# Four long bursts of compression matmuls in place of nine short ones, between the k-tiles of an NSA projection

## The reference

```python
L_CMP = 32
def nsa_project(h, w_in, pos):
    z = h @ w_in                      # D_MODEL = 1024 in, q, kc, vc, ks, vs, kw, vw and gates out
    ...
def nsa_compress(k, pe, w):           # k: (B, L, NSA_KV, NSA_DH)
    blk = k.reshape(B, L // L_CMP, L_CMP, NSA_KV, NSA_DH) + pe[:, None, :]
    return jnp.einsum('bclgd,lde->bcge', blk, w)
```

## Time and profile before

| what | value |
|---|---|
| median of 3 runs | 3520.2 us |
| profiled execution | 3519.06 us |
| span of its trace | 3517.4 us |
| PE busy | 3184.3 us (91%) |
| DVE, ACT, POOL busy | 1839.1, 1292.3, 386.6 us |
| mean granted TensorE clock | 0.957 |
| DMA | 339.10 MB, mean 96 GB/s |

### The profile page before, as it was taken

One profiled execution on the slowest core, in us unless ns is written; L12 is line 12 of the kernel. 1 busy time (PEld: TensorE's weight loads), 2 busy tenths in 40 slices (PEclk: granted clock), 3 DMA queues, 4 the chain that ended last, 5 costly groups with the idle time before them and its releaser, 6 DMA issues. The chain is left out here.

```text
span 3517.4 us, 71223 instructions
## 1 busy us (share of the span) xinstructions
PE 3184.3 (91%) x29474; PEld 2946.8 (84%) x29474; DVE 1839.1 (52%) x3124; ACT 1292.3 (37%) x2225; POOL 386.6 (11%) x266
## 2 busy tenths in 40 slices
PE   7988889999889678778999898999989989889997
PEld 6875579999789678668999897999988855789997
DVE  2136636546489654436636484764622256356363
ACT  3236524323355323024323374432322256343232
POOL 2222110000134000020000032000012221200000
PEclk9999999999999899789999999999999999999999
DMA  6634222232222000214222322323265443042322
GB/s 188 198 112 165 93 101 88 84 105 72 67 77 74 5 0 0 84 66 149 80 101 83 85 90 84 111 84 102 74 142 167 142 163 115 31 149 75 105 83 67
DMA packets 146424, 339.10 MB, mean 96 GB/s; under 512 B 58212, under 2 KB 84452, under 8 KB 132468
## 3 DMA queue, kind: packets, MB, share of 16 engines
q1 hardware_dynamic: 137204, 296.03, 26.4%
q0 software_dynamic: 7424, 37.76, 2.9%
q10 hardware_dynamic: 1536, 1.60, 0.2%
HBM read 318.40 MB, written 32.12 MB: 100 GB/s over the span
## 5 line engine op out<-in xcount | busy, mean ns | idle before, releaser
L357 PE MATMUL ffn_ps<-ffn_x_hi_sb,ffn_w_hi_sb 128*128 128x260 f32 x2816 | 571.9, 284 | 40.8 <-DVE ffn_x_lo_sb L165 37.5
L357 PE MATMUL ffn_ps<-ffn_x_hi_sb,ffn_w_lo_sb 128*128 128x260 f32 x2816 | 569.5, 284 | 0.0
L357 PE MATMUL ffn_ps<-ffn_x_lo_sb,ffn_w_hi_sb 128*128 128x260 f32 x2816 | 568.8, 284 | 0.0
L357 PEld LDWEIGHTS ffn_ps<-ffn_x_hi_sb,ffn_w_hi_sb 128*128 128x128 f32 x2816 | 436.7, 190 | 46.1 <-issue 35.8
L357 PEld LDWEIGHTS ffn_ps<-ffn_x_hi_sb,ffn_w_lo_sb 128*128 128x128 f32 x2816 | 436.4, 189 | 0.0
L357 PEld LDWEIGHTS ffn_ps<-ffn_x_lo_sb,ffn_w_hi_sb 128*128 128x128 f32 x2816 | 435.4, 189 | 0.0
L397 ACT ACTIVATE ffn_w_hi_sb<-ffn_raw_sb 128x2048 fp32r<-128x2048 f32 (+2 forms) x152 | 256.9, 1690 | 349.1 <-PE ffn_ps L357 349.1
L449 DVE TENSOR_TENSOR ffn_w_lo_sb<-ffn_raw_sb,ffn_w_hi_sb 128x2048 fp32r<-128x2048 f32 (+2 forms) x152 | 305.1, 2007 | 47.3 <-ACT ffn_w_hi_sb L397 47.3
L415 ACT ACTIVATE ffn_pre_sb<-ffn_ps 128x520 f32<-128x520 f32 x176 | 106.6, 606 | 605.4 <-PE ffn_ps L357 315.9
L464 DVE SCALAR_TENSOR_TENSOR ffn_conv_sb<-ffn_pre_sb,ffn_conv_w_sb,ffn_conv_sb 128x512 f32<-128x512 f32 x176 | 132.3, 752 | 344.9 <-ACT ffn_conv_sb L417 344.9
L357 PE MATMUL ffn_ps<-ffn_inner_hi_sb,ffn_w_hi_sb 128*128 128x260 f32 x1408 | 283.9, 283 | 6.5 <-DVE ffn_inner_lo_sb L482 3.4
(11 more groups left out here) (451 smaller groups left out, 6335.4 us busy)
## 6 DMA issues: line engine op xcount, KB each, us to landing
ffn_raw_sb<-ffn_w_in SPq DMA_DIRECT2D x88, 1024.0 KB, 4.9
ffn_raw_sb<-ffn_w_out SPq DMA_DIRECT2D x32, 768.0 KB, 4.3
nsa_ring_sb<-sel_pages SPq DMA_DIRECT2D x160, 128.0 KB, 2.5
ffn_raw_sb<-ffn_w_out SPq DMA_DIRECT2D x32, 640.0 KB, 3.9
nsab_w_raw_sb<-nsa_w_in SPq DMA_DIRECT2D x32, 512.0 KB, 5.3
nsab_page_slot_sb<-cmp_pages SPq DMA_DIRECT2D x64, 256.0 KB, 3.9
all_xn_t_sb<-cmp_pages SPq DMA_DIRECT2D x64, 256.0 KB, 3.6
gdnp_w_raw_sb<-gdn_w_in SPq DMA_DIRECT2D x32, 512.0 KB, 3.9
```

The costliest lines, as they stand in the source:

```text
L357: mm = pe.matmul(psf[:, bank + h, 0:H], wp[:, w[0], w[1]:w[1] + P], xp[:, h * H:(h + 1) * H], start=start and k == 0, stop=stop and k == 2)
```

## The change

The number of compression steps that shall be done by k-tile `step` (0 to 10) of group n was a straight line from step 1 to step 10, and becomes four equal jumps of eight:

```diff
--- before.py
+++ after.py
@@ -1754,7 +1754,7 @@
                     if u >= FIRST:
                         n, step = (u - FIRST) * KT + kt, 0
                         n, step = n // STEPS, n % STEPS
-                        compress_to(32 * n + max(0, step - 1) * 32 // (STEPS - 2))
+                        compress_to(32 * n + 8 * sum(step >= at for at in (3, 5, 8, 10)))
```

## The result

The changed kernel takes 3499.24 us, median of six runs (3496.48 to 3503.0), against 3520.46 us (3518.35 to 3525.12, six runs). The ratio is 0.9938 with a 95% interval of [0.9926, 0.9951]: 21.2 us less, where 28 were forecast. The median lies 0.2 us above the upper end of the stated range (3499). The profiled execution took 3496.48 us (span 3494.8), 22.6 us less than the profiled one of before.

A forecast was written before the change was run, and what follows sets the result against it. The prediction took PE (TensorE) to bound the stretch: 80 fewer switches at 0.357 us save 28.6 us, less a 0.65 us page wait gives 27.95 us, so 3492.0 us from a median of 3520.2, range 3489 to 3499.

The forecast's parts named there:

- PE bounds the stretch: Units 5 to 15 of both NSA projections: PE busy 119.19 of 119.63 and 118.58 of 118.86 us, so its savings count.
- The price of a switch, 0.357 us: Each compression burst between projection k-tiles: fixed 0.357 us for switching there and back, whatever the burst's length.
- The term of 28.6 us: Compression bursts in both layers: 80 fewer, at 0.357 us each, save 28.6 us.
- Longer bursts keep their pace: Bursts of 64 matmuls in the trace: still 0.117 us a compression step, 1.10 us to the next projection matmul.
- Weights and ACT's copies don't bind: Shorter units: weight loads hold 5.74 us a unit, shortest unit 8.3 us; ACT gets 0.72 us more for copies.
- A page wait of 0.65 us: Group 5's first burst: sample 4's last page late, 0.35 us in layer 0 plus 0.3 in layer 3; bounds 0 to 4.
- the third rival: Long bursts starve PE of instructions: last 8 matmuls slow to 120 ns, 46.6 us lost, 3539 us; chance 0.05.
- The range: Whole kernel: 3489 (full 28.6 us, cheaper remaining switches) to 3499 us (4 us page bound, first half of page pile-up).

The follow-up runs named there:

- e1: Kernel before (nine bursts per group), page loads of samples 2 to 7 cut to 64 of 512 columns: 3516.62 us, ratio 0.9992.
- e2: Changed kernel (four bursts of eight steps), page loads of samples 2 to 7 cut to 64 of 512 columns: 3487.71 us, ratio 0.9913.
- e13: Changed kernel with its four bursts of eight steps behind k-tiles 2, 5, 8, 10 instead of 3, 5, 8, 10: 3494.98 us, ratio 0.9921.
- e8: Changed kernel with one burst of 32 steps per group and pages of samples 2 to 7 cut to 64 of 512 columns: 3510.36 us, ratio 0.9969.
- e4: Changed kernel with one burst of 32 steps per group, behind k-tile 10, full pages: 3520.7 us, ratio 1.0008.
- e9: Changed kernel with pages of samples 2 to 7 issued one by one, each after a given k-tile, all bytes loaded: 3496.41 us, ratio 0.9928.
- e12: Changed kernel with bursts behind k-tiles 2, 5, 8, 10 and the layer-key store issued behind sample 4's second half of pages: 3495.83 us, ratio 0.9925.
- e14: Changed kernel with five bursts of six or seven steps, behind k-tiles 2, 4, 6, 8, 10: 3497.6 us, ratio 0.9933.
- e7: Changed kernel with each compression matmul on the whole array instead of a 64x64 quarter, read from the timeline alone: 3948.83 us.
- e3: Changed kernel with two bursts of sixteen steps per group, behind k-tiles 5 and 10, full pages: 3505.04 us, ratio 0.9956.

## Why the prediction was nearly right

- *PE bounds the stretch, so what it saves is saved.* Right: 22.4 of 22.6 us of the gain stand in the stretch.
- *The price of a switch, 0.357 us, read from k-tiles with and without a burst.* Right, by e1 and e2 (0.361 and 0.356), and the same at eight steps as at three. The term of 28.6 us stands; with light pages 28.9 us were measured.
- *Longer bursts keep their pace.* Right for the pace: 1.10 us for x64.
- *Weights and ACT's copies don't bind.* Right: no such wait is new.
- *A page wait of 0.65 us.* Not seen. It was covered: pages of sample 4 landed at 135.94 in layer 0 by the DMA records, and PE asked at 136.31, having lost 0.94 us at 132.97. Without that pause it would have asked 0.57 us too soon, where 0.35 us was booked. In layer 3 they landed at 2703.03, and PE asked at 2706.22, behind 3.8 us of pauses since group 3's end. That the cover did it is worked out, not tried; e13 shows the wait itself.
- *The step that failed is the third rival.* It was given 0.05 and priced as a slower pace at the end of each burst. Its kind was right (PE short of instructions) and its form wrong. PE pauses at block borders, a few times a layer, where a fetch takes longer than the 256 instructions ahead of it last. In the changed kernel that cost 7.3 us by the distances from start to start, less the usual distance at the place, against 1.0 us before; the windows against e2's and e1's say the same (2.85 + 4.47 and 0.90 + 0.13 us). That is 6.3 us more, and 28.6 - 6.3 = 22.3 us, where the stretches show 22.4. The term that the sum lacked is this one: it had nothing for late instructions.
- *The range.* Its upper end was built from page waits that never came; that the time came out next to it, with another loss in their place, is luck.
- *The evidence lay in the rows.* The 0.3 us of "issue" in the earlier trace rows was such a pause (it ended at 75.46, 1.26 us behind an instruction packet). I took it for noise instead of asking how near the other borders were to it.

Left open: how much of a late block is the fetch's own length and how much other traffic. Traffic matters (by their ratios e2 is some 9 us under the changed kernel, 0.9913 against 0.9938, and has no idle PE in the stretch; e8 is some 14 us under e4), and the draw matters with little traffic (e8). That the pages' clumps are the harmful part of the traffic is not borne out by e9. How much e4's lower clock adds to its pauses wasn't separated. Weights, stores and swaps go through the same queues and were not varied, but for the one store that e12 moves.

## What to carry to other kernels

Compare the start distances of the same work with and without a foreign burst in it, over bursts of two lengths: the part that doesn't grow with length is the price of the switch, and it scales with the number of bursts until something else binds. Before making bursts longer, count PE's instructions, weight loads too. In e8 a block drawn in 1.9 us brought a pause of 1.8 us; in the kernel before, where the 256 instructions ahead of a pause lasted 5.2 to 6.0 us, the three pauses took 0.2 to 0.5 us. Where a block would be drawn much faster than that with DMA busy, expect pauses put to "issue", and put slow work (few instructions a microsecond) evenly between; e13 and e14 speak for it, e12 doesn't. The best number of bursts here lies between the ends, at four or five, and not at nine or one.

## What the runs showed of the hardware

- A change between 64x64 quarters and the whole array costs, in and out together, 0.36 us (e1 against e2); using the whole array in the burst leaves some 0.08 us of it (e7).
- A compression matmul of fp32 in the program is two matmuls and two weight loads in the trace, and they count as four instructions: with that count the pauses fall on multiples of 256.
- PE went on 1.2 to 1.6 us after the end of the instruction packet that it waited for, in 40 cases of 40 (changed kernel, e3, e4).
- With the pages of samples 2 to 7 cut to an eighth the same four bursts had no such pause (e2, PE busy 104.29 of 104.29 and 104.49 of 104.49 us).
